# Squares of the first token half added in pairs, the first unit multiplied lot by lot, weight sums ahead of a convolution tail

## The reference

```
h    = rmsnorm(x, norm1_g)
proj = h @ w_in            # split into b_a, c_a, v_a, v_b (1024 each), g_a, g_b (2048 each)
u    = causal_depthwise_conv3(c_a * v_a)         # 3 taps and a bias
y_a  = (b_a * u) @ w_a_out
p    = trailing_mean(v_b) - v_b                  # windows 2, 4, 8, 16 by channel group
y_b  = per_group_linear(p) * pool_scale
x    = x + (sigmoid(g_a + b) * y_a + sigmoid(g_b + b) * y_b) @ w_o
x    = x + (silu(h2 @ w_ffn_gate) * (h2 @ w_ffn_up)) @ w_ffn_down,   h2 = rmsnorm(x, norm2_g)
out  = rmsnorm(x, final_g)
```

## Time and profile before

| | |
|---|---|
| median of 3 runs | 1507.72 us (1507.36 to 1509.26) |
| profiled execution | 1508.08 us |
| its span, slowest core | 1506.5 us |
| spans of the cores | 1499.8 to 1506.5 us |
| granted TensorE clock | 0.986, core 7 0.990 |
| TensorE busy | 1445.9 us, 96% |
| VectorE, ScalarE, POOL busy | 71%, 19%, 18% |

### The profile page before, as it was taken

One profiled execution on the slowest core, in us unless ns is written; L12 is line 12 of the kernel. 1 busy time (PEld: TensorE's weight loads), 2 busy tenths in 40 slices (PEclk: granted clock), 3 DMA queues, 4 the chain that ended last, 5 costly groups with the idle time before them and its releaser, 6 DMA issues.

```text
span 1506.5 us, 19996 instructions; the slowest of 8 cores (1499.8 to 1506.5 us)
## 1 busy us (share of the span) xinstructions
PE 1445.9 (96%) x6885; PEld 650.0 (43%) x6885; DVE 1071.3 (71%) x1665; ACT 290.6 (19%) x475; POOL 276.4 (18%) x288
## 2 busy tenths in 40 slices
PE   8999999899999999999999999999999999999993
PEld 3444444344444444444444344434443444444441
DVE  2767887766676778766777887788778876886454
ACT  3611011121122123330011111111111111111143
POOL 0210000000000026730000320032003200320065
PEclk9999999999999999999999999999999999999997
DMA  9745435366556577554455455545554555455525
GB/s 235 146 72 85 84 56 78 53 86 94 79 82 90 86 194 170 84 82 76 75 90 91 76 81 90 90 75 81 91 91 74 81 90 92 77 81 90 89 58 202
DMA packets 26162, 143.04 MB, mean 95 GB/s; under 512 B 3024, under 2 KB 3280, under 8 KB 11472
## 3 DMA queue, kind: packets, MB, share of 16 engines
q0 software_dynamic: 17568, 116.40, 49.9%
q1 hardware_dynamic: 8496, 25.37, 5.1%
HBM read 249.77 MB, written 8.39 MB: 171 GB/s over the span
## 4 chain that ended last, share of the span: by engine, by line
PE 89%; issue 3%; DVE 3%; POOL 2%; DMA 1%; ACT 1%; POOLq 0%; DVEq 0%; SPq 0%; ACTq 0%
PE ps L416 74%; PE ps L619 9%; DVE arena L397 3%; PE ps L1251 2%; PE ps L1166 2%; PE ps L566 2%; POOL arena L397 2%; DMA arena<-x_t 1%; PE ps L590 1%; ACT arena L407 0%; DVE arena L403 0%; ACT ps L407 0%; PE ps L549 0%; ACT L407 0%; POOLq L251 0%
## 5 line engine op out<-in xcount | busy, mean ns | idle before, releaser
L416 PE MATMUL ps<-arena 128*128 128x512 bf16 x5360 | 1173.3, 381 | 30.1 <-DVE arena L397 28.7
L416 PEld LDWEIGHTS ps<-arena 128*128 128x128 bf16 x5360 | 522.1, 98 | 677.6 <-issue 65.1
L397 DVE TENSOR_TENSOR arena<-ps,arena 128x512 f32<-128x512 f32 (+2 forms) x660 | 451.6, 699 | 274.5 <-PE ps L416 196.6
L397 DVE TENSOR_TENSOR arena<-arena 128x1024 bf16<-128x1024 bf16 (+6 forms) x713 | 480.1, 708 | 18.6 <-ACT arena L407 6.0
L397 POOL TENSOR_TENSOR arena<-arena 128x512 f32<-128x512 f32 (+1 forms) x162 | 210.9, 1315 | 224.6 <-DVE arena L397 164.1
L437 POOL DMA_DIRECT2D arena<-wpack x105 | 56.9, 542 | 821.6 <-PE ps L416 547.3
L400 ACT COPY arena<-ps 128x512 f32<-128x512 f32 (+1 forms) x134 | 74.0, 560 | 438.1 <-PE ps L416 348.5
L619 PE MATMUL ps<-arena 128*128 128x512 bf16 x640 | 140.2, 379 | 2.7 <-POOL arena L397 2.2
L407 ACT ACTIVATE arena<-arena 128x512 f32<-128x512 f32 (+1 forms) x139 | 86.0, 625 | 246.1 <-DVE arena L397 203.2
L397 DVE TENSOR_TENSOR arena<-arena,ps 128x512 f32<-128x512 f32 x106 | 72.6, 684 | 69.4 <-PE ps L416 69.3
L619 PEld LDWEIGHTS ps<-arena 128*128 128x128 bf16 x640 | 62.1, 98 | 79.5 <-issue 6.7
(11 more groups left out here) (28 smaller groups left out, 110.7 us busy)
## 6 DMA issues: line engine op xcount, KB each, us to landing
arena<-wpack POOLq DMA_DIRECT2D x106, 1024.0 KB, 9.6
arena<-x_t SPq DMA_DIRECT2D x8, 1024.0 KB, 15.2
arena<-x_t SPq DMA_DIRECT2D x16, 512.0 KB, 14.2
out<-arena SPq DMA_DIRECT2D x32, 256.0 KB, 3.2
arena<-wpack POOLq DMA_DIRECT2D x16, 320.0 KB, 4.9
arena<-x_t SPq DMA_DIRECT2D x1, 128.0 KB, 2.6
prm<-sparams SPq DMA_DIRECT2D x1, 64.0 KB, 2.7
pos_sb<-pos SPq DMA_DIRECT2D x1, 8.0 KB, 11.9
```

Of the source, the lines that this page charges most:

```text
L397: em.op(eng, lambda e: e.tensor_tensor(out=out, in0=a, in1=b, op=op), reads, writes)
L416: ins = e.matmul(out, lhs(k), rhs(k), start=(start and k == 0), stop=(k == n - 1), skip_group_check=True)
```

## The change

In the first stage, the squares of each two blocks are added by VectorE, in place, ahead of one ones-matmul, which leaves 8 of 16. The filler matmuls between the lots go, and the filler ahead of the first lot grows from 20 to 28 matmuls. Unit 0's matmuls on half 0 run in four parts of 8, each after its lot. The second weight issue waits for lot 1 instead of lot 2. `std_ew(0, 0, 0, 1)` moves ahead of the `scale1` of blocks 4 to 7. At the change to Strassen, `hsum(BSPEC[1])` comes before unit 4's halo and first product, `prep(6)` with three of its sums and `hsum(BSPEC[2])` come before `cv_ew(0, 1, 7, 0)`, and what is left of the queue is pumped in two parts of two.

```diff
             issue()
-            em.wait_tokens("pool", r_xs[2].w)
+            em.wait_tokens("pool", r_xs[1].w)
             issue()
...
             ones_mm(bank(7)[:, 0:16], sqh[:, 0:16], True, True, [R["sqh"]], [r_bank[7]])
-            warm(20)
+            warm(28)
...
             for b in range(NB):
+                i = b % 5
                 xs_bf(0, b, "dve")
-                sq(0, b, sqr[b % 5], r_sqr[b % 5])
-                ones_mm(bank(6), sqr[b % 5], b == 0, b == NB - 1, [r_sqr[b % 5]], [r_bank[6]])
-                if b % 4 == 3 and b < 12:
-                    warm(5)
+                sq(0, b, sqr[i], r_sqr[i])
+                if b % 2:
+                    i0 = (b - 1) % 5
+                    tt(sqr[i], sqr[i], sqr[i0], ALU.add, [r_sqr[i], r_sqr[i0]], [r_sqr[i]])
+                    ones_mm(bank(6), sqr[i], b == 1, b == NB - 1, [r_sqr[i]], [r_bank[6]])
+                if b % 4 == 3:
+                    pl_mm(0, (0, 1), *smv(0), b - 3, b + 1)
             rfac(S1, r_S1, 0, 6)
             halo_mm(0, 5)
-            pl_mm(0, (0, 1), *smv(0))
             halo_mm(1, 5, 32)
             pl_mm(1, (2, 3), *smv(0))
...
             pq(0)
+            std_ew(0, 0, 0, 1)
             for b in range(4, 8):
                 scale1(0, b)
-            std_ew(0, 0, 0, 1)
             pq(1)
...
             pl_mm(4, (7, 0), *hmv(1))
             issue()
+            hsum(BSPEC[1])
             halo_cv(6, 0)
             cv_ew(0, 0, 4, 5)
             pump(2)
-            hsum(BSPEC[1])
             halo_mm(5, 6, 32)
             pl_mm(5, (1, 2), *hmv(0))
+            prep(6)
+            pump(3)
+            hsum(BSPEC[2])
             cv_ew(0, 1, 7, 0)
             conv_tail(2, 0)
-            prep(6)
-            hsum(BSPEC[2])
+            pump(2)
             pl_mm(5, (3, 4), *hmv(1))
             issue()
             halo_cv(6, 1, 32)
             cv_ew(1, 0, 1, 2)
-            pump(4)
+            pump(2)
             cv_ew(1, 1, 3, 4)
             hsum(BSPEC[3])
             hsum(BSPEC[4])
```

## The result

The changed kernel took **1500.0 us** (median of 5 runs) against 1508.9 for the kernel before, now also of 5 runs. The ratio is 0.9945, with a 95% interval of 0.9931 to 0.9958: 8.3 us faster, 6.3 to 10.4. The forecast was 8.2 us. The profiled execution ran 1501.7 us.

What follows compares the result with a forecast made beforehand. TensorE, busy 96% of the span, was taken to bound the kernel. Gains of 7.0 us in the first stage and 1.2 at Strassen, clock 0, made -8.2 from the 1507.7 median: 1499.5 us, range 1496.0 to 1503.5.

Steps and rivals of the forecast that it cites:

- Part 1: First-stage lots: squares added in pairs drop 8 of 16 ones-matmuls, freeing 7.0 us of TensorE, fillers 3.2 more; VectorE just covered.
- Part 2: First lots: unit 0 multiplied lot by lot, 3.5 us per lot; `rfac` at 31.6, 33.4 if clock falls.
- Part 3: Unit 1's weights issued earlier: unit 1 lands at 36.1, lot 3 27.5, lot 4 36.5; 24 matmuls start 7.0 us sooner.
- Rival A: Unit 1's weights cut into lot 3, which lands at 32.6, `rfac` at 36.6; total 1502.7 us; chance 0.15.
- The halo wait: VectorE's wait for unit 1's halo matmuls, ahead of its second-half additions, ends at 37.0 instead of 44.92.
- The second half: Second token half: ScalarE ends at 53.8, VectorE at about 53; the 24 matmuls start at 54.1 instead of 61.10.
- Clock at the start: First lots: if the clock falls as before, `rfac` and lot 3's multiplication come 1.8 us later, 33.4 and 35.0.
- `std_ew` at nothing: Second half on VectorE: moving `std_ew` ahead of four `scale1` costs nothing, at worst 1 us if a cast waits.
- Part 4: Change to Strassen: weight sums made early shorten the 2.88 us idle before unit 6's fifth product; gain 1.2 us.
- The clock at 0: TensorE's clock after its idles, such as unit 6's: effect of shorter idles taken as 0, bounds 1.7 us either way.
- Rival B: From 44 to 54 us clock holds at half between ScalarE's bursts; 1518 us if all, 1511 if two thirds; chance 0.06.
- Rival C: x cuts up unit 1, landing at 44 or later; only the 1.2 us at Strassen left, 1506.5 us; chance 0.08.

Runs made afterwards that it cites:

- part 4 alone: Only the weight sums moved ahead of the convolution tail at the change to Strassen, on the kernel before; 0.9979 of before, 3.2 us less.

## Why the prediction was right, point by point

Each part's size came out. The path by which the second half got there was partly another, and two of the agreements are luck, as said below.

- **Part 1.** TensorE had 3.44 us per lot (forecast 3.5). Confirmed by leaving the pairs out: 5.16 us per lot and 3.9 us lost. VectorE was just covered, as forecast, until the last lot: where lot 3's landing set the pace, `rfac` came 4.9 us after it, and I had 4.1.
- **Part 2.** `rfac` at 32.9, between the forecast's 31.6 (clock kept) and 33.4 (clock lost). Cores 1 and 6 of the changed kernel are the two cases, 31.7 and 34.6; core 6 lies past the upper value, as it lost 3.2 us of clock there and not 1.8.
- **Part 3.** On core 6 unit 1 landed at 35.4, lot 3 at 26.4 (17.1 + 9.3; forecast 27.5), lot 4 at 35.1; over all cores lot 3 landed at 25.6 to 28.3. Shifting the whole pattern of sharing by 3 us was right to 1.4 us in the median. Rival A's size (lot 3 at 32.6) is out, but its kind is there: lot 4 came 4 us later with the early issue than with the late one, and lot 3 came 1.3 us later than before and set `rfac` on four cores. "1 to 2 us of idle ahead of unit 1" was wrong for most cores: TensorE finished the lots later than I had it, and only cores 1, 5 and 4 waited (1.46, 0.62 and 0.19 us).
- **The halo wait.** The number was right (36.9 for 37.0), the path to it was not. I let unit 1's landing end it. On seven of eight cores `rfac` and three `scale1` did: 32.9 + 4.0. With the 31.6 to 33.4 that I had for `rfac`, that path gives 35.6 to 37.4, and I hadn't worked it out. That both paths end at nearly the same time is luck.
- **The second half.** The number was right, the mechanism partly not. I let ScalarE set 53.8 and VectorE 53. In fact ScalarE would have allowed about 53 (it started at 35.3 and had no waits of note), and VectorE, the step I had as covered, set 54.3. What I missed is that VectorE's 16.0 us of work was measured beside another alignment with POOL. Before, one of POOL's two multiplications fell into VectorE's wait for the halo (43.95) and the other, at 49.90, met instructions that read PSUM; now they meet additions of two SBUF tiles, and these took 1.11 and 1.78 us for 0.69, 1.5 us together. By the start of the 24 matmuls (0.3 us after the last cast) I had ScalarE at 54.1 and VectorE at 53.3; they were at about 53 and 54.3. Two errors of about 1 us offset each other, and that the 7.0 came out as 6.9 is luck to that extent.
- **Clock at the start.** The 7.0 us are taken from core 4's rows, which hold 1.8 us of clock lost in the first lots. I used that loss for the bounds of `rfac` but not in the gain. About 2.4 of the 6.9 us hang on it.
- **`std_ew` at nothing.** It cost about 0.5 us (53.8 without the move), of the 1 us allowed, by the meetings with POOL and not by a cast that waits.
- **Part 4.** 1.1 us for the forecast 1.2, by the instructions named.
- **The clock at 0.** Right as a sum, of -1.35 at unit 6 and +1.37 at unit 12, which I had not foreseen.
- **Rival B** (the clock holds at half between bursts) did not happen: from 36 to 60 us the granted clock was 1.00 on all eight cores. **Rival C** fell with unit 1's landing, 34.2 to 35.7 us on the eight cores.

## What to carry to other kernels

A filler or a deferred block of matmuls is the first place to look for time while transfers arrive: real work that is ready goes into the lots, but only if the next unit's transfer is moved up by as much, since neither alone gained anything over the pairs (56.6 and 58.2 for 55.9 at the 24 matmuls). When a wait is shortened, ask which engine comes last now: here the halo wait gave way to `rfac`, at nearly the same time. When one engine's stretch is moved against another's, its busy time doesn't simply move with it: ask which of its instructions will now run beside the other engine. And read a shortened idle together with the next one downstream, because a clock saved at one wait was lost at the other.

## What was not expected of the hardware

- **A VectorE addition of two SBUF tiles is held until POOL's multiplications are over; instructions that read PSUM are not.** In one execution of the changed kernel (core 6) POOL multiplied at 46.33 for 1.26 us, and the addition of two SBUF tiles at 46.36 took 1.78 us instead of 0.69. Later POOL does five multiplications back to back:

```profile
66.59 6.17 POOL L397 TENSOR_TENSOR arena<-arena 128x512 bf16<-128x512 f32 x5
69.59 3.73 DVE L397 TENSOR_TENSOR arena<-arena 128x512 f32<-128x512 f32 x1
```

The addition began during the third and ended at 73.32, 0.56 us after the fifth. In all 24 cases of the changed kernel (three on each core) such an addition ended 0.54 to 0.56 us after POOL's multiplications. So the price is what POOL still has to do in one go when the addition starts, and it can be more than one instruction. With `std_ew` back, casts of one SBUF tile were held in the same way (1.50 us for 0.48, ended 0.3 us after POOL). In the kernel before (core 4), POOL multiplied from 49.90 and VectorE's two multiplications with a PSUM operand from 49.69 took 1.28 us together, no more than elsewhere. With POOL's two multiplications in the stretch taken away the additions there are back at 0.69. The Trainium skill (GPSIMD Engine Reference, section on specifications) says that POOL shares its SBUF interfaces with VectorE and contends with VectorE instructions that have two SBUF inputs or run in a 2-port performance mode. The trace agrees for the additions; whether the casts ran in such a mode no trace here shows.
- **The length of an idle alone doesn't decide whether the clock is lost.** After 1.75 us of idle at unit 6 it was lost on none of eight cores, after 1.72 us ahead of unit 2 on four of eight of the changed kernel, and after 2.64 us at unit 12 on two of eight (before) or eight of eight (part 4 alone).
